# Moving two groups of transposes ahead of a matmul level in a bidirectional state scan

## The chip, the cores and the metric

The kernel runs on one core of a Trainium2 chip. The metric is the device time of one execution in microseconds. The kernel before takes 1659.57 us (median of three executions, 1650.67 to 1659.82).

## What is computed

Two transformer-like blocks follow each other on 512 tokens of width 1024, in float32. The change touches only the first block's mixer. That mixer holds a recurrence of the RWKV kind over 8 heads of width 64, run forwards and backwards over the tokens, after 256 context tokens have gone through the same recurrence:

```
def wkv_scan(state0, r, decay, kk, b, v, k, reverse):
    def step(S, inp):
        r_t, w_t, kk_t, b_t, v_t, k_t = inp
        sa = jnp.einsum("bhvk,bhk->bhv", S, kk_t)
        S = (S * w_t[:, :, None, :] - sa[..., None] * b_t[:, :, None, :]
             + v_t[..., None] * k_t[:, :, None, :])
        return S, jnp.einsum("bhvk,bhk->bhv", S, r_t)
```

Everything else (modulation, norms, the projections, two gated feed-forward networks with depthwise convolutions, and in the second block a gated linear recurrence and a sliding-window attention) is the same in both kernels.

## The kernel before, in words

The program is written by hand for each engine: TensorE (PE), VectorE (DVE), ScalarE (ACT), GpSimd (POOL) and SyncE each have one list of instructions in program order, and semaphores stand between them. Nothing reorders these lists.

The recurrence is computed in chunks of L = 64 tokens: NCC = 4 chunks of context and NCX = 8 of the sequence, NC = 12 in all, in two directions d = 0 and 1 that don't depend on each other. Within a chunk a 64 x 64 triangular system has to be inverted. That is done by doubling: levels l = 2 to 6, each of them a short chain that goes back and forth between PE and DVE:

- `nx(m, d, l)`: 8 matmuls of 64x64 by 64x32 (16 MATMUL instructions in the trace, since a float32 product is issued as two), which wait for X of the level before;
- `w_out(m, d, l)`: DVE masks the product from PSUM into w (L2214);
- `dx(m, d, l)`: again 16 MATMUL instructions, which wait for w and Y;
- `x_out(m, d, l)` (L2221): DVE adds the product to X, and `x_turned(m, d, l)` (L2228) transposes X into Y. The next level's `nx` waits for X alone, its `dx` for Y and w.

The loop at the centre of the change is `for n in range(-2, NC)`, which each engine's list contains. In iteration n three chunks are in work: chunk n is finished (`state_in`, `updates`, `state_terms`, from chunk NCC on `results`), chunk m = n + 1 is inverted (the levels), and chunk q = n + 2 is prepared (`scores_b`, `scores_k`). In iterations -1 to 6 a piece of another computation runs beside it, a matrix-vector product for the modulation: `ada_parts` (L967, 64 MATMUL instructions on the whole array), a copy by ACT, `ada_select` (L978, 8 MATMUL instructions) and one DVE addition into `mod` (L2305).

`turned(m, d)` transposes chunk m's two 64 x 64 blocks per head, `bh` and `kh`, by 16 matmuls against the identity (32 MATMUL instructions, out<-in `bank<-k_,arena`). It waits for `kr` of chunk m, which DVE wrote in the iteration before. Its results are copied by ACT (`tok_out`, L1575) and are used by `state_terms` in the next iteration. POOL may overwrite `bh` and `kh` with chunk q's only after `turned(m, d)` (`done("tok_mm", d, q)`): POOL's L1944 makes the new `bh` in two steps, L1930 multiplies `bh` and, from chunk 4 on, `rt`; `scores_b(q, d)` waits for both.

On PE, iteration n has this order around the change (level 3 only; the next level begins with `nx(m, d, 4)`):

```
state_terms(n, 0), state_terms(n, 1)
nx(m, 0, 3), nx(m, 1, 3)
turned(m, 0)
dx(m, 0, 3), dx(m, 1, 3)
ada_select(n)                      # n = -1 to 6
turned(m, 1)
results(n, 0), results(n, 1)       # n = 4 to 11
nx(m, 0, 4), nx(m, 1, 4), dx(m, 0, 4), dx(m, 1, 4), nx(m, 0, 5), nx(m, 1, 5)
```

`turned` exists for m = 0 to 10, which is n = -1 to 9; in n = 10 level 3 already stands without it. Levels 4 and 5 have no other work between `nx(4)`, `dx(4)` and `nx(5)`. On DVE, `state_out(n)` (L2264, L2266), which adds the state terms and waits for `state_terms`, stands ahead of `w_out(m, d, 3)`.

In iterations 0 to 7 SyncE also issues the weight pieces of `ada_parts`, paced by waits for the counts of `nx` and `dx` of direction 0.

Of the kernel before, what the change touches and what calls it, by code (L numbers as in the profile page):

```python
# [32 lines left out]
NC = NCC + NCX  # L33
# [137 lines left out]
def two_blocks(nc, xT, ctxT, vec, con, band, w8, w11, lora, gup, outT):  # L171
    with ExitStack() as ctx:
# [88 lines left out]
        def vcol(name, *shape):  # L261
            o, w = VEC[name]
            a = v[:, o:o + w]
            if not shape:
                return a
            names = " ".join(f"d{i}" for i in range(len(shape)))
            return a.rearrange(f"p ({names}) -> p {names}", **{f"d{i}": n for i, n in enumerate(shape)})
# [9 lines left out]
        def spread(a, *shape):  # L277

            return a.unsqueeze(len(a.shape)).broadcast_to([P, *shape])
# [305 lines left out]
        def _(pe):  # L585
# [185 lines left out]
            def done(name, d, count):  # L771

                if count > 0:
                    pe.wait_ge(s[f"{name}{d}"], count)
# [93 lines left out]
            def turned(m, d):  # L868

                sc = scans[d]  # L870
                done("kr", d, m + 1)
                for k, src in enumerate((sc.bh, sc.kh)):
                    last = tiles(lambda j, r: bank[d][1][r, NJ * L * k + L * j:NJ * L * k + L * j + L],
                                 lambda j, r: src[r, j, :], lambda j, r: ident[r, r])
                last.then_inc(s[f"tok_mm{d}"], 1)
# [23 lines left out]
            def state_terms(n, d):  # L899

                sc = scans[d]
                done("gu", d, 2 * n + 2)
                done("tok", d, n + 1)
                v_in = v_tok[:, place(d, n) // L]
                for j in range(NJ):
                    out = bank[d][3][:, L * j:L * j + L]
                    for r in HALVES:
                        mm(out[r], sc.tok[r, 0, j, :], sc.gu[r, j, :], start=True, stop=False)  # L908
                    for r in HALVES:
                        last = mm(out[r], sc.tok[r, 1, j, :], v_in[r, j, :], start=False, stop=True)  # L910
                last.then_inc(s[f"ds_mm{d}"], 1)
# [60 lines left out]
            def ada_select(n):  # L972

                pe.wait_ge(s["ada_row"], 8 + n + 2)
                done("nr", 1, n + 2)
                for u in range(2):
                    for c in range(2):
                        last = mm(banks[4][:, 4 * u + 2 * c:4 * u + 2 * c + 2], ada_row2[:, u, :], select[:, c, :],  # L978
                                  start=True, stop=True)
                last.then_inc(s["ada_turned"], 1)  # L980

            both = (0, 1)
            for n in range(-2, NC):
                m, q = n + 1, n + 2
                inv, prep, ada = 0 <= m < NC, q < NC, -1 <= n < 7
                if n >= 0:
                    for d in both:
                        state_in(n, d)
                if inv:
                    for d in both:  # L990
                        nx(m, d, 2)
                if n >= 0:
                    for d in both:
                        updates(n, d)
                if inv:
                    for d in both:
                        dx(m, d, 2)
                if ada:
                    ada_parts(n)
                if 0 <= n < NC - 1:  # L1000
                    for d in both:
                        state_terms(n, d)
                if inv:
                    for d in both:
                        nx(m, d, 3)
                if 0 <= m < NC - 1:
                    turned(m, 0)
                if inv:
                    for d in both:
                        dx(m, d, 3)  # L1010
                if ada:
                    ada_select(n)
                if 0 <= m < NC - 1:
                    turned(m, 1)
                if n >= NCC:
                    for d in both:
                        results(n, d)
                if inv:
                    for d in both:
                        nx(m, d, 4)  # L1020
                    for d in both:
                        dx(m, d, 4)
                    for d in both:
                        nx(m, d, 5)
                if prep:
                    for d in both:
                        scores_b(q, d)
                if inv:
                    for d in both:
                        dx(m, d, 5)  # L1030
                if prep:
                    scores_k(q, 0)
                if inv:
                    for d in both:
                        nx(m, d, 6)
                if prep:
                    scores_k(q, 1)
                if inv:
                    for d in both:
                        dx(m, d, 6)  # L1040
# [966 lines left out]
        def _(dve):  # L2007
# [182 lines left out]
            def done(name, d, count):  # L2190

                if count > 0:
                    dve.wait_ge(s[f"{name}{d}"], count)
# [22 lines left out]
            def x_out(m, d, l):  # L2216
                sc = scans[d]
                done("dx_mm", d, 5 * m + l - 1)
                add = bank[d][2][:, 128:256].rearrange("p (b t) -> p b t", t=1 << l - 1)
                early = sides(sc.X, l, d)  # L2220
                V.tensor_tensor(early, add, early, ALU.add).then_inc(s[f"X{d}"], 1)  # L2221

            def x_turned(m, d, l):
                sc = scans[d]
                done("X", d, 5 * m + l)
                if l == 2:
                    done("gu_mm", d, 2 * m)
                V.transpose(flat(sc.Y), flat(sc.X)).then_inc(s[f"Y{d}"], 1)  # L2228
# [48 lines left out]
            both = (0, 1)  # L2277
            dve.wait_ge(s["gate"], 2 * NJ)
            dve.wait_ge(s["presets"], 8)
            for n in range(-2, NC):  # L2280
                m, q = n + 1, n + 2
                inv, prep, ada = 0 <= m < NC, q < NC, -1 <= n < 7
                if inv:
                    for d in both:
                        w_out(m, d, 2)
                if prep:
                    for d in both:
                        running_sums(q, d)
                if inv:
                    for d in both:  # L2290
                        x_out(m, d, 2)
                        x_turned(m, d, 2)
                if 0 <= n < NC - 1:
                    state_out(n)
                if inv:
                    for d in both:
                        w_out(m, d, 3)
                if inv:
                    for d in both:
                        x_out(m, d, 3)  # L2300
                        x_turned(m, d, 3)
                if ada:
                    at = 16 + 4 * (n + 1)
                    dve.wait_ge(s["ada_turned"], n + 3)
                    V.tensor_tensor(mod[:, at:at + 4, :], banks[4][:, 0:8].rearrange("p (m c) -> p m c", c=2),  # L2305
                                    spread(vcol("adab")[:, at:at + 4], 4, 2), ALU.add).then_inc(s["mod"], 1)
                if n >= NCC + NCX // 2:
                    for d in both:
                        second_result(n, d)
                if inv:  # L2310
                    for d in both:
                        w_out(m, d, 4)
                    for d in both:
                        x_out(m, d, 4)
                        x_turned(m, d, 4)
                    for d in both:
                        w_out(m, d, 5)
                if prep and q >= NCC:
                    for d in both:
                        scores_out(q, d, 0)  # L2320
                if inv:
                    for d in both:
                        x_out(m, d, 5)
                    for d in both:
                        x_turned(m, d, 5)
                if prep:
                    for d in both:
                        first_level(q, d)
                if inv:
                    for d in both:  # L2330
                        w_out(m, d, 6)
                if prep:
                    for d in both:
                        first_turned(q, d)
                    scores_out(q, 0, 1)
                if inv:
                    for d in both:
                        y_last(m, d)
                if prep:
                    scores_out(q, 1, 1)  # L2340
# [483 lines left out]
```

## Time and profile before

| | |
|---|---|
| Device time, median of 3 | 1659.57 us |
| Lowest and highest of the 3 | 1650.67 and 1659.82 us |
| The profiled execution's own time | 1659.57 us |
| Its span in the profile | 1657.6 us |
| Scan loop (n = -2 to 11) in the trace | about 268 to 560 us |
| Mean granted TensorE clock over the span | 0.962 of full speed |

The span is what the profile covers, first to last instruction; the execution's own time is 2.0 us longer. A matmul's row starts when it is issued and ends when its last result is modelled to be out, so matmuls overlap: a small matmul's row here lasts about 0.22 us while the next one starts some 0.03 us later. A TensorE that is shown busy can therefore still lose a tenth of a microsecond between two instructions, and such losses are read from how long a given count of instructions takes. The granted clock is given as a share of full speed, 0.50 or 1.00 at any moment.

### The profile page before, as it was taken

The numbers are of one execution on the slowest core, as the hardware profiler recorded it, in microseconds if no ns is written. First come the engines' busy times: TensorE is split into PE (matmuls) and PEld (weight loads), VectorE is DVE, ScalarE is ACT, GpSimd is POOL, SyncE is SP. The second block draws the span as 40 slices with busy tenths as digits, with TensorE's granted clock in tenths as the row PEclk, the third lists the DMA queues.
The fourth block names the chain that finished last, engine by engine and source line by source line (L and its number), as shares of the span: only waits on it lengthen the run. The fifth ranks groups of instructions, "written<-read, shape, count | busy, mean of one in ns | idle before, by whom it ended". The sixth has DMA issues, their size and how long they took to land.

```text
span 1657.6 us, 36556 instructions
## 1 busy us (share of the span) xinstructions
PE 1571.5 (95%) x15540; PEld 1324.2 (80%) x15540; DVE 885.0 (53%) x1417; ACT 572.7 (35%) x987; POOL 219.5 (13%) x230
## 2 busy tenths in 40 slices
PE   7899998999999978999999999999979999999997
PEld 3787886999999766778777887777867788888886
DVE  1624213665566445888887224667454556555222
ACT  3422334332232223434443223535544222323221
POOL 0000002333233010111111121000001011111111
PEclk8899997999999988999999998999979999999999
DMA  8242100332210121222222232221102222222221
GB/s 340 77 147 77 51 26 8 99 106 92 81 42 4 53 77 52 98 79 102 101 81 107 88 104 76 82 79 57 46 26 98 80 93 86 100 101 95 90 102 68
DMA packets 38750, 139.74 MB, mean 84 GB/s; under 512 B 3040, under 2 KB 3552, under 8 KB 38112
## 3 DMA queue, kind: packets, MB, share of 16 engines
q1 hardware_dynamic: 38480, 135.76, 23.4%
q8 instruction: 104, 1.70, 0.4%
q10 hardware_dynamic: 144, 2.10, 0.3%
q14 instruction: 22, 0.18, 0.0%
HBM read 135.75 MB, written 2.10 MB: 83 GB/s over the span
## 4 chain that ended last, share of the span: by engine, by line
PE 86%; DVE 8%; ACT 3%; issue 1%; DMA 0%; POOL 0%; DVEq 0%; SPq 0%; ACTq 0%
PE bank L647 58%; PE bank L780 12%; DVE ffn_sb L2471 2%; PE bank L657 2%; PE bank L967 1%; PE bank L610 1%; PE bank L886 1%; PE bank L908 1%; PE bank L888 1%; PE bank L592 1%; PE bank L1285 1%; PE bank L910 1%; ACT arena L1752 1%; DVE w_in L2091 1%; PE bank L1256 1%
## 5 line engine op out<-in xcount | busy, mean ns | idle before, releaser
L647 PE MATMUL bank<-hf_hi,w_up 128*128 128x512 f32 x1376 | 424.9, 390 | 0.0
L647 PEld LDWEIGHTS bank<-hf_hi,w_up 128*128 128x128 f32 x1376 | 259.1, 188 | 53.6
L647 PE MATMUL bank<-hf_lo,w_up 128*128 128x512 f32 x688 | 271.2, 394 | 4.8 <-DVE w_up L2091 4.3
L647 PE MATMUL bank<-act_hi,w_down 128*128 128x512 f32 x704 | 216.8, 389 | 0.0
L780 PE MATMUL bank<-arena 64*64 64x32 f32 (+2 forms) x4992 | 177.0, 227 | 8.5 <-POOL arena L1930 7.6
L780 PEld LDWEIGHTS bank<-arena 64*64 64x64 f32 x4992 | 170.6, 137 | 13.2 <-issue 8.7
L1403 ACT ACTIVATE w_up<-ring 128x1024 fp32r<-128x1024 f32 x88 | 93.0, 1058 | 215.9 <-PE bank L647 215.9
L2091 DVE TENSOR_TENSOR w_up<-ring,w_up 128x1024 fp32r<-128x1024 f32 x88 | 108.0, 1229 | 105.3 <-ACT w_up L1403 105.2
L647 PEld LDWEIGHTS bank<-hf_lo,w_up 128*128 128x128 f32 x688 | 129.5, 188 | 39.4 <-DVE w_up L2091 13.2
L2471 DVE SCALAR_TENSOR_TENSOR ffn_sb<-ffn_sb 128x512 f32<-128x512 f32 x176 | 151.5, 861 | 5.5
L647 PEld LDWEIGHTS bank<-act_hi,w_down 128*128 128x128 f32 x704 | 132.2, 188 | 27.4
L647 PE MATMUL bank<-act_lo,w_down 128*128 128x512 f32 x352 | 137.1, 389 | 1.3 <-DVE w_down L2097 1.3
L2091 DVE TENSOR_TENSOR w_in<-ring,w_in 128x1024 fp32r<-128x1024 f32 x48 | 58.5, 1223 | 139.9 <-ACT w_in L1403 139.7
L1988 POOL TENSOR_TENSOR act_lo<-ffn_sb,act_hi 128x512 f32 x44 | 72.9, 1656 | 443.5 <-ACT act_hi L1681 429.8
L647 PE MATMUL bank<-hx_hi,w_in 128*128 128x512 f32 x384 | 120.4, 395 | 0.0
L647 PE MATMUL bank<-h_hi,w_in 128*128 128x512 f32 x320 | 98.8, 390 | 0.0
L2097 DVE TENSOR_TENSOR w_down<-ring,w_down 128x1408 fp32r<-128x1408 f32 x32 | 52.1, 1628 | 86.8 <-ACT w_down L1420 86.8
L1403 ACT ACTIVATE w_in<-ring 128x1024 fp32r<-128x1024 f32 x48 | 50.4, 1055 | 138.9 <-PE bank L647 130.9
L1420 ACT ACTIVATE w_down<-ring 128x1408 fp32r<-128x1408 f32 x32 | 44.2, 1381 | 155.6 <-PE bank L647 155.6
L647 PEld LDWEIGHTS bank<-hx_hi,w_in 128*128 128x128 f32 x384 | 73.7, 192 | 15.3
L647 PE MATMUL bank<-hx_lo,w_in 128*128 128x512 f32 x192 | 76.7, 400 | 5.4 <-ACT arena L1478 3.6
L647 PEld LDWEIGHTS bank<-act_lo,w_down 128*128 128x128 f32 x352 | 66.1, 188 | 15.4 <-DVE w_down L2097 1.8
(319 smaller groups left out, 2364.8 us busy)
## 6 DMA issues: line engine op xcount, KB each, us to landing
ring<-w SPq DMA_DIRECT2D x76, 1024.0 KB, 4.7
ring<-w SPq DMA_DIRECT2D x32, 704.0 KB, 4.0
ring<-w SPq DMA_DIRECT2D x64, 256.0 KB, 2.9
arena<-w SPq DMA_DIRECT2D x2, 3072.0 KB, 22.6
x<-xT SPq DMA_DIRECT2D x1, 2048.0 KB, 11.8
arena<-w SPq DMA_DIRECT2D x2, 1024.0 KB, 20.3
x<-xT ACTq DMA_DIRECT2D x1, 2048.0 KB, 8.9
outT<-x SPq DMA_DIRECT2D x4, 512.0 KB, 2.7
```

The costliest lines, as they stand in the source:

```text
L592: last = mm(out[32 * q:32 * q + 32, :].rearrange("r (c m) -> r c m", c=2), siluc[:, 2 * q + k, :], w[:, :, 2 * q + k, :], start=k == 0, st ...
L610: last = mm(bank[:, 0:t], ones, sq[:, k, :], start=k == 0, stop=k == KB - 1)
L647: ins = mm(out, w[:, a, k, :], of_block(b, k0 + k), start=first and k == 0 and m == 0, stop=last and k == n - 1 and m == 2)
L657: ins = mm(out, w[:, a, k, :], of_block(b, k), start=k == 0 and m == 0, stop=k == KB - 1 and m == 2)
L780: last = mm(out(j, r), lhs(j, r), rhs(j, r), start=True, stop=True)
L886: mm(out[r], sc.ktrt[r, n % 3, j, 0:L], sc.S[r, n % 2, j, :], start=True, stop=False)
L1403: act_f(w[:, 0], slot_view(g)[:, at:at + blocks, :], ACT.Copy).then_inc(s["w_hi"], 1)
L1420: act_f(w_down[half][:, 0], slot_view(g, HALF), ACT.Copy).then_inc(s["w_hi"], 1)
L1988: nc.gpsimd.tensor_tensor(act_lo[:, bass.ds(j, 1), :].rearrange("p a t -> p (a t)"), silu[u], act_hi[:, bass.ds(j, 1), :].rearrange("p a t ...
L2091: V.tensor_tensor(w[:, 1], slot_view(SLOT[name] + u)[:, c * KB:c * KB + KB, :], w[:, 0], ALU.subtract).then_inc(s["w_lo"], 1)
L2097: V.tensor_tensor(w[:, 1], slot_view(SLOT[name] + half, HALF), w[:, 0], ALU.subtract).then_inc(s["w_lo"], 1)
L2471: ins = V.scalar_tensor_tensor(to, pad[u][:, n // 3:n // 3 + GRID_H, n % 3:n % 3 + GRID_W], tap_w[u][:, n:n + 1], to, ALU.mult, ALU.add)
```

## The change

On PE both `turned` groups now stand ahead of `nx(m, d, 3)`, and `ada_select` stands between `nx(m, 1, 3)` and `dx(m, 0, 3)`. On DVE the addition into `mod`, which waits for `ada_select`, moves ahead of `x_out(m, d, 3)` accordingly. Nothing is added or removed; no wait is changed.

```
--- before.py
+++ after.py
@@ -1000,18 +1000,17 @@
                 if 0 <= n < NC - 1:
                     for d in both:
                         state_terms(n, d)
+                if 0 <= m < NC - 1:
+                    for d in both:
+                        turned(m, d)
                 if inv:
                     for d in both:
                         nx(m, d, 3)
-                if 0 <= m < NC - 1:
-                    turned(m, 0)
-                if inv:
-                    for d in both:
-                        dx(m, d, 3)
                 if ada:
                     ada_select(n)
-                if 0 <= m < NC - 1:
-                    turned(m, 1)
+                if inv:
+                    for d in both:
+                        dx(m, d, 3)
                 if n >= NCC:
                     for d in both:
                         results(n, d)
@@ -2295,15 +2294,15 @@
                 if inv:
                     for d in both:
                         w_out(m, d, 3)
-                if inv:
-                    for d in both:
-                        x_out(m, d, 3)
-                        x_turned(m, d, 3)
                 if ada:
                     at = 16 + 4 * (n + 1)
                     dve.wait_ge(s["ada_turned"], n + 3)
                     V.tensor_tensor(mod[:, at:at + 4, :], banks[4][:, 0:8].rearrange("p (m c) -> p m c", c=2),
                                     spread(vcol("adab")[:, at:at + 4], 4, 2), ALU.add).then_inc(s["mod"], 1)
+                if inv:
+                    for d in both:
+                        x_out(m, d, 3)
+                        x_turned(m, d, 3)
```

The list of PE in iteration n = 0, from the end of `state_terms` (L908 and L910) to the `state_in` after it. `bank<-arena 64x32` rows are `nx` and `dx` (8 matmuls a direction), `bank<-k_,arena` is `turned`, L978 is `ada_select`, the last two `64x64` and `64x32` rows belong to `scores` and the later levels:

```order
 L908 MATMUL bank<-arena 64x64 x2
 L910 MATMUL bank<-x,arena 64x64 x2
-L780 MATMUL bank<-arena 64x32 x16
-L780 MATMUL bank<-k_,arena 64x64 x16
+L780 MATMUL bank<-k_,arena 64x64 x32
 L780 MATMUL bank<-arena 64x32 x16
 L978 MATMUL bank<-k_,x 128x2 x4
-L780 MATMUL bank<-k_,arena 64x64 x16
-L780 MATMUL bank<-arena 64x32 x48
+L780 MATMUL bank<-arena 64x32 x64
 L780 MATMUL bank<-arena 64x64 x16
 L780 MATMUL bank<-arena 64x32 x16
```

Both transpose groups (x16 each) now stand as one x32 ahead of level 3. Between `nx(3)` and `dx(3)` there is `ada_select`, and from `dx(3)` on 64 matmuls of the levels stand in one row, with nothing between `dx(3)`, `nx(4)`, `dx(4)` and `nx(5)`.

The list of PE in iteration n = 7, which has no `ada_select` but has `results` (L923 and on), in the kernel before:

```order
L780 MATMUL bank<-arena 64x32 x16
L780 MATMUL bank<-k_,arena 64x64 x16
L780 MATMUL bank<-arena 64x32 x16
L780 MATMUL bank<-k_,arena 64x64 x16
L923 MATMUL bank<-arena 64x64 x2
```

and in the kernel after:

```order
L780 MATMUL bank<-k_,arena 64x64 x32
L780 MATMUL bank<-arena 64x32 x32
L923 MATMUL bank<-arena 64x64 x2
```

Here `nx(3)` and `dx(3)` have become one row of 32 with nothing between them; `results` still follows `dx(3)`.

The list of DVE in an iteration with `ada`, from `w_out(3)` to `w_out(4)`, in the kernel before (line 2305 is the addition into `mod`):

```order
L2214 TENSOR_TENSOR arena<-bank,k_ 128x128 [waits nx_mm0]
L2214 TENSOR_TENSOR arena<-bank,k_ 128x128 [waits nx_mm1]
L2221 TENSOR_TENSOR arena<-bank,arena 128x32x4 [waits dx_mm0]
L2228 STREAM_TRANSPOSE arena<-arena 128x256 [waits X0]
L2221 TENSOR_TENSOR arena<-bank,arena 128x32x4 [waits dx_mm1]
L2228 STREAM_TRANSPOSE arena<-arena 128x256 [waits X1]
L2305 TENSOR_TENSOR mod<-bank,v 128x8 [waits ada_turned]
L2214 TENSOR_TENSOR arena<-bank,k_ 128x128 [waits nx_mm0]
```

and in the kernel after (its lines are one to five lower in number):

```order
L2213 TENSOR_TENSOR arena<-bank,k_ 128x128 [waits nx_mm0]
L2213 TENSOR_TENSOR arena<-bank,k_ 128x128 [waits nx_mm1]
L2300 TENSOR_TENSOR mod<-bank,v 128x8 [waits ada_turned]
L2220 TENSOR_TENSOR arena<-bank,arena 128x32x4 [waits dx_mm0]
L2227 STREAM_TRANSPOSE arena<-arena 128x256 [waits X0]
L2220 TENSOR_TENSOR arena<-bank,arena 128x32x4 [waits dx_mm1]
L2227 STREAM_TRANSPOSE arena<-arena 128x256 [waits X1]
L2213 TENSOR_TENSOR arena<-bank,k_ 128x128 [waits nx_mm0]
```

The addition into `mod` went from behind level 3's transposes to ahead of its `x_out`. ACT's, POOL's and SyncE's lists are the same in both kernels.

## Rows read from the trace of the kernel before

**Rows 1.** The page's first lines: span, busy time by engine.

```profile
span 1657.6 us, 36556 instructions
...
PE 1571.5 (95%) x15540; PEld 1324.2 (80%) x15540; DVE 885.0 (53%) x1417; ACT 572.7 (35%) x987; POOL 219.5 (13%) x230
```

**Rows 2.** The page's chain that ended last, by engine.

```profile
PE 86%; DVE 8%; ACT 3%; issue 1%; DMA 0%; POOL 0%; DVEq 0%; SPq 0%; ACTq 0%
```

**Rows 3.** Windows: whole scan, iterations n = 0, 7 and 10.

```profile
core 0: us, PE busy (x) PEld busy (x) DVE busy (x) ACT busy (x) POOL busy (x), PEclk, DMA share, GB/s
268.00:560.00 292.00, 283.06 (x8512) 276.22 (x8512) 174.62 (x509) 91.21 (x266) 93.54 (x136) 0.97 0.19 62
299.80:321.33 21.53, 21.53 (x687) 20.92 (x685) 13.13 (x43) 7.95 (x23) 6.97 (x10) 1.00 0.32 103
467.60:490.18 22.58, 22.58 (x712) 22.39 (x710) 14.83 (x43) 7.32 (x22) 8.20 (x12) 1.00 0.06 16
535.50:557.00 21.50, 21.00 (x682) 20.31 (x680) 11.78 (x37) 2.68 (x7) 0.00 (x0) 1.00 0.02 5
```

**Rows 4.** Waits of PE in the scan, 268 to 560 us.

```profile
PE bank L780 <- POOL arena L1930: 7.6, 2, 6.9
```

**Rows 5.** Timeline of iteration n = 0, PE and DVE: start, us, instruction, [idle before].

```profile
308.38 1.07 PE L780 MATMUL bank<-arena 64*64 64x32 f32 x32
...
309.06 0.42 DVE L2266 TENSOR_TENSOR arena<-arena 128x256 f32<-128x256 f32 x1
...
309.40 0.48 DVE L2214 TENSOR_TENSOR arena<-bank,k_ 128x128 f32<-128x128 f32 x2
...
311.25 1.05 PE L978 MATMUL bank<-k_,x 128*128 128x2 f32 x8
...
312.35 0.17 DVE L2305 TENSOR_TENSOR mod<-bank,v 128x8 f32<-128x8 f32 x1
...
313.87 0.29 DVE L2214 TENSOR_TENSOR arena<-bank,k_ 128x128 f32<-128x128 f32 x1 [1.36 <-PE bank L780]
...
314.34 0.29 DVE L2214 TENSOR_TENSOR arena<-bank,k_ 128x128 f32<-128x128 f32 x1 [0.17 <-PE bank L780]
...
314.92 0.29 DVE L2221 TENSOR_TENSOR arena<-bank,arena 128x128 f32<-128x128 f32 x1 [0.29 <-PE bank L780]
315.25 0.45 DVE L2228 STREAM_TRANSPOSE arena<-arena 128x256 f32<-128x256 f32 x1
315.62 0.25 DVE L2221 TENSOR_TENSOR arena<-bank,arena 128x128 f32<-128x128 f32 x1
...
315.91 0.45 DVE L2228 STREAM_TRANSPOSE arena<-arena 128x256 f32<-128x256 f32 x1
316.27 0.65 DVE L2214 TENSOR_TENSOR arena<-bank,k_ 128x128 f32<-128x128 f32 x2
```

**Rows 6.** Windows of PE: level 3, then levels 4 and 5; n = 0, 2, 7.

```profile
core 0: us, PE busy (x), PEclk, DMA share, GB/s
308.36:311.12 2.76, 2.76 (x104) 1.00 0.30 99
313.20:316.39 3.19, 3.19 (x104) 1.00 0.33 116
356.77:360.10 3.33, 3.33 (x104) 1.00 0.37 125
474.17:476.93 2.76, 2.76 (x103) 1.00 0.03 9
480.70:483.88 3.18, 3.18 (x104) 1.00 0.02 5
```

**Rows 7.** Timeline of POOL in iteration n = 2.

```profile
357.05 0.73 POOL L1944 TENSOR_TENSOR arena<-arena 128x256 f32<-128x256 f32 x1 [2.24 <-PE bank L780]
357.86 2.69 POOL L1930 TENSOR_TENSOR arena<-arena 128x256 f32<-128x256 f32 x4
```

**Rows 8.** Windows of PE, n = 10: level 3, then `nx(4)` and `dx(4)`.

```profile
541.90:544.20 2.30, 2.02 (x72) 1.00 0.00 0
547.04:549.00 1.96, 1.96 (x72) 1.00 0.03 8
```

**Rows 9.** Windows at the low clock: start of the scan, and later.

```profile
279.30:282.83 3.53, 3.53 (x70) 3.48 (x66) 2.29 (x6) 0.58 (x3) 0.16 (x1) 0.50 0.02 5
...
1199.00:1209.00 10.00, 9.25 (x43) 8.02 (x43) 4.66 (x14) 9.25 (x17) 0.00 (x0) 0.50 0.01 2
```

More of the change, by code:

```diff
@@ L1005, in _ @@
                         nx(m, d, 3)
-                if 0 <= m < NC - 1:
-                    turned(m, 0)
+                if ada:
+                    ada_select(n)
                 if inv:
@@ L1010, in _ @@
                         dx(m, d, 3)
-                if ada:
-                    ada_select(n)
-                if 0 <= m < NC - 1:
-                    turned(m, 1)
                 if n >= NCC:
```

## The prediction

> **What bounds the kernel now.** I read the page's first lines, then the chain that ended last, then the scan alone in windows, then one iteration instruction by instruction. TensorE is shown busy for 1571.5 of 1657.6 us [rows 1] and holds 86% of the chain that ended last [rows 2]; VectorE, busy for 53%, holds 8%. The change lies in the scan, 268 to 560 us, where TensorE is busy for 283.06 of 292.00 us; iterations n = 0 and n = 7 show it busy for their whole 21.53 and 22.58 us, at a granted clock of 1.00 [rows 3]. The list of waits in the scan has one large entry, 7.6 us for POOL in two waits, one of them 6.9 us [rows 4]. This stands at the scan's start, before the first `turned`, and the change doesn't touch it. So the scan goes at the pace of TensorE's list. A change of order can win only what TensorE loses between instructions, and that does not show as idle time, since a matmul's row outlasts its issue by 0.2 us. It has to be read from how long equal counts of instructions take.
>
> There the profile is clear. In n = 0 the 96 instructions of level 3 (`nx`, `turned(m, 0)`, `dx`) take 2.76 us; the 96 of `nx(4)`, `dx(4)`, `nx(5)`, which have nothing between them, take 3.19 us [rows 6] (both windows count 104, since 8 earlier rows reach in). Iteration 7 gives 2.76 and 3.18 us. At 2.76/96 = 0.029 us an instruction, the covered level loses nothing, and the uncovered stretch loses 0.43 us in three joints. Level 3 is already covered today; the transposes cannot be a better cover for it than they are. What they leave, they uncover.
>
> **What an uncovered joint costs.** VectorE's rows in n = 0 split the 0.43 us [rows 5]. The two `w_out(4)` start at 313.87 and 314.34, 0.47 us apart, which is one direction's 16 instructions. The two `x_out(4)` start at 314.92 and 315.62, 0.70 us apart, because direction 0's transpose (315.25, 0.45 us) stands between them. `nx(5)` of direction 1 waits for the second, which ends at 315.87, 0.66 us after the first ended at 315.21. Its turn on TensorE would come after 0.47 us, so 0.19 us is lost there. The other 0.43 - 0.19 = 0.24 us is the way PE to DVE and back, once after `nx(4)` and once after `dx(4)`: 0.12 us each. So a bare joint from `nx` to `dx` costs 0.12 us, and a bare joint from `dx` to the next `nx` costs 0.12 + 0.19 = 0.31 us.
>
> **The change part by part.**
>
> *`nx(3)` to `dx(3)`.* Before, `turned(m, 0)` stood there. After, in n = -1 to 6 `ada_select` does: it takes about 1.0 us (its row starts at 311.25, the next group's work follows one microsecond later) [rows 5], against the 0.12 us that has to be covered. Nothing is lost, 8 times. In n = 7, 8 and 9 nothing stands there: 3 x 0.12 = +0.36 us. In n = 10 there was no `turned`, and nothing changes.
>
> *`dx(3)` to `nx(4)`.* Before, `ada_select` and `turned(m, 1)` stood there. After, from n = 4 on `results` does, 96 instructions or about 2.8 us by the rate above: covered. In n = -1 to 3 nothing does: 5 x 0.31 = +1.55 us.
>
> *`nx(4)` to `dx(4)` in the same five iterations.* VectorE now comes to `w_out(4)` from level 3's transposes without a break. What that is like stands in the rows one level on [rows 5]: after the transpose at 315.91 the next `w_out` starts at 316.27, 0.65 us after `x_out` of direction 1 began at 315.62. `nx` of that direction starts at about 315.93 (0.06 us after 315.87) and takes 0.47 us, so TensorE is free at 316.40; the first mask is done at 316.27 + 0.29 = 316.56, and with 0.06 us to TensorE `dx` could start at 316.62. There `scores_b` hides this; at level 4 it would show 0.22 us in place of 0.12. Five times 0.10 makes +0.50 us, and the rest of level 4 is as before.
>
> *The transposes themselves.* They cost the same instructions. Their wait, `kr` of chunk m, was fulfilled in the iteration before. In their new place they delay `nx(3)` by 64 x 0.029 = 1.9 us, which nobody but the levels waits for. `state_out` on VectorE, which ends at 309.48 in n = 0 (309.06 + 0.42) right when `w_out(3)` begins [rows 5], now lies under the transposes; there was no stall behind it to win, since level 3 took 2.76 us.
>
> *POOL.* The new `bh` needs both transposes done. `turned(m, 1)` moves about 3 us earlier (the 16 + 16 instructions of `nx` and of `dx` and `ada_select`: 0.93 + 0.93 + 1.0 us), so POOL's work for the next chunk ends earlier. This wins in n = 2 and 3 alone, where `rt` is wanted and no `results` gives POOL time: in n = 2 POOL takes up direction 1's `bh` at 357.05 and is in its four multiplications until 360.55 [rows 7], and the stretch up to `scores_b` takes 3.33 us in place of 3.19 [rows 6]. 2 x 0.14 = -0.28 us.
>
> *The addition into `mod` on VectorE.* It took 0.17 us at 312.35, right after `ada_select` [rows 5]. In its new place it is done while `dx(3)` of direction 0 is still issuing (0.47 us). Behind it wait `x_out(3)` and so `nx(4)`; they need `dx(3)`, which comes later anyway. Cost nothing; it would cost up to 0.17 us in each of 8 iterations, 1.4 us, if that cover were missing.
>
> *SyncE.* Two of the eight paced pieces in an iteration wait for `nx` or `dx` of level 3 and go out about 2 us later; the last ones wait for level 6 and go as before. As the slots are wanted only after the last, nothing.
>
> Sum: 0.36 + 1.55 + 0.50 - 0.28 = +2.1 us. The profiled execution took 1659.57 us, which is also the median of the three; its span is 1657.6 and 2.0 us lie around it. So 1659.57 + 2.1 = 1661.7 us.
>
> Bounds. Below: if no joint shows and only POOL's gain does, -0.3 us. Above: n = 10 is the worst joint of this level in the trace. There `nx(3)` and `dx(3)` stand bare behind `state_terms` and the same 64 instructions take 2.30 us in place of 1.96 for level 4's, which itself loses 0.12 [rows 8], so 0.46 us. If each of the 8 iterations with a new bare joint cost 0.46 at `nx` to `dx`, on top of 0.31 + 0.10 in five of them, it would be 3.7 + 2.0 = +5.7 us. I take the 0.12, because in n = 10 VectorE is held up by `state_out`, and after the change 1.9 us of transposes stand between. With the 1.4 us of the addition, +7.1 us is the upper end.
>
> **The rivals.**
>
> *Only the gain shows.* For it: the waits are tenths of a microsecond, and the profile's list shows none of them. Against it: rows 6 show the loss at levels 4 and 5 in each iteration that I looked at. Time: 1659.3 us.
>
> *The clock falls, and it is slower.* TensorE's rows in n = -1 to 3 would break more often, and if its granted clock fell to the low of its two levels (1.2 in place of 2.4 GHz) there, an instruction of the scan would take 3.53 us for 64 (0.055 us) in place of 0.029 [rows 9]. Later in the kernel such a stretch lasts at least from 1199 to 1209 us [rows 9]; 10 us of it holds work for about 5.3, so it costs 4.7 us. One in each of the five iterations makes +23.5 + 2.1 us: 1685 us. It decides from four such stretches on: 18.8 + 2.1 is over 1%. Against it: iteration 10 has the 0.46 us stall and 0.5 us of idle time in 21.50, and its clock reads 1.00 [rows 3], as do all those with levels 4 and 5 bare.
>
> The Trainium skill speaks for this rival (page "TensorE: Matmul & The Clock Gate", section "A second HAM failure mode: psum-queue depth-cycling"): where TensorE idles for moments between groups of matmuls often enough, its clock goes back and forth and the throughput suffers. This trace bears it out for this kernel's scan so far in no iteration: the clock is 1.00 in rows 3 with three such joints in each. By that rule the time would be this rival's.
>
> *The runs' own spread.* One execution of three was 8.9 us shorter than the other two. The low clock in some later stretches [rows 9] can fall otherwise when the scan ends 2 us later. If the lower value becomes the usual one: 1650.7 + 2.1 = 1652.8 us.
>
> *More is won than I see, over 1%.* For that TensorE would have to lose 16.6 us over 11 iterations, 1.5 us in each, at the places that are now filled. Level 3 took 2.76 us for 96 instructions, as fast as the list can go. I find no room for it.
>
> **How the numbers follow.** My case has 0.77, the lower value of the spread 0.12, only the gain 0.05, the clock 0.03, the upper bound near 1667 another 0.03. The likeliest case gives 1661.7 us. For 8 in 10 the range must hold my case with its bounds (1659.3 to 1666.7), and reach down to the lower value: 1652 to 1667 us. About 1% (16.6 us) is what a measurement of this kernel can tell from no change. Faster by over 1% (under 1643): 0.01. Slower by over 1% (over 1676): 0.04, the clock and what I overlook. The same: 0.95.
>
> **What would show it right or wrong.** Right: in n = 0 to 3 the 64 instructions from `dx(3)` to `nx(5)` show a bare joint more, seen in VectorE's second `x_out(3)` starting 0.7 us after the first, and in `w_out(4)` right behind the second transpose; those iterations get 0.3 to 0.45 us longer, n = 4 to 6 stay, n = 7 to 9 get 0.12 longer, and n = 2's stretch up to `scores_b` loses its extra 0.14 us. POOL's L1944 of direction 1 comes about 3 us earlier. Wrong: a granted clock under 1.00 between 290 and 555 us; VectorE's addition into `mod` ending after `dx(3)` of direction 0; `dx(3)` of n = 7 waiting longer than 0.15 us; or the scan getting shorter.

## The result, and the profile after

The changed kernel takes 1675.7 us (median of four executions, 1670.06 to 1682.14), beside 1658.67 us for the kernel before in the same comparison. The ratio is 1.0111, with a 95% interval of 1.0072 to 1.0151: about 1.1% slower, outside the range that I gave. Over all of its 35 executions it took between 1663.97 and 1686.08 us, with a median of 1674.9.

The page of the changed kernel, its first lines and its chain by engine:

```profile
span 1672.3 us, 36556 instructions
...
PE 1585.7 (95%) x15540; PEld 1337.8 (80%) x15540; DVE 888.0 (53%) x1417; ACT 573.6 (34%) x987; POOL 219.4 (13%) x230
...
PE 89%; DVE 7%; ACT 3%; issue 1%; DMA 0%; POOL 0%; SPq 0%; DVEq 0%; ACTq 0%
```

Against [rows 1, 2] the span grew by 14.7 us and TensorE's busy time by 14.2 us, with the same 15540 instructions. So it is not TensorE's shown idle time that grew. Either its instructions take longer, or there are more of the short waits that hide inside its rows. The list of TensorE's waits in the scan shows no new one, since its large entry is that of [rows 4]:

```profile
PE bank L780 <- POOL arena L1929: 7.6, 2, 6.9
```

The iterations n = -1 to 8 of the changed kernel, in windows of PE (us, busy with its count, granted clock, DMA):

```profile
279.79:302.15 22.36, 22.36 (x524) 0.72 0.27 83
302.15:326.47 24.32, 24.32 (x687) 0.86 0.29 89
326.47:352.57 26.10, 26.01 (x686) 0.80 0.27 84
352.57:378.74 26.17, 26.17 (x686) 0.87 0.28 86
378.74:402.00 23.26, 23.26 (x686) 1.00 0.32 95
402.00:427.69 25.69, 25.69 (x783) 1.00 0.27 86
427.69:453.37 25.68, 25.68 (x782) 1.00 0.28 86
453.37:481.02 27.65, 27.58 (x782) 0.94 0.27 79
481.02:504.18 23.16, 23.02 (x710) 1.00 0.06 16
504.18:526.88 22.70, 22.70 (x710) 1.00 0.02 4
```

and of the kernel before, n = -1 to 3 and n = 8:

```profile
279.35:299.82 20.47, 20.47 (x524) 0.80 0.28 91
299.82:321.36 21.54, 21.54 (x687) 1.00 0.32 103
321.36:343.12 21.76, 21.72 (x687) 1.00 0.31 100
343.12:366.41 23.29, 23.29 (x687) 1.00 0.29 95
366.41:389.45 23.04, 23.04 (x688) 1.00 0.29 95
...
490.20:512.78 22.58, 22.58 (x710) 1.00 0.02 5
```

The reader should look at the clock. In n = 0, 1 and 2 it was 1.00 and is 0.86, 0.80 and 0.87, and these three iterations got 2.8, 4.3 and 2.9 us longer; n = -1 went from 0.80 to 0.72 and got 1.9 us longer. Where the clock stayed at 1.00, the change costs what the waits cost: +0.22 us in n = 3 and +0.12 us in n = 8. The four iterations n = -1 to 2 hold 11.9 of the 14.7 us. Of the later ones, n = 6, with a clock of 0.94, takes 27.65 us against 25.68, n = 7 takes 0.6 us more at a clock of 1.00, and n = 4 takes 25.69 where the kernel before takes 26.80, of which TensorE is shown idle for 0.54.

Windows just before such a fall and behind it, in n = 0 and n = 1 of the changed kernel:

```profile
314.00:316.00 2.00, 2.00 (x52) 1.95 (x51) 0.86 (x4) 2.00 (x7) 1.73 (x3) 1.00 0.47 139
316.30:323.00 6.70, 6.70 (x126) 6.70 (x128) 2.92 (x9) 0.77 (x2) 1.90 (x3) 0.50 0.49 157
338.00:340.00 2.00, 2.00 (x46) 1.94 (x43) 0.75 (x3) 2.00 (x7) 1.92 (x4) 1.00 0.34 89
340.30:350.20 9.90, 9.90 (x190) 9.90 (x190) 4.95 (x16) 1.26 (x4) 2.29 (x4) 0.50 0.40 122
```

TensorE was shown busy throughout, at the high of its two levels, with `ada_select`, `dx(3)` and the start of `nx(4)` in n = 0, and with `nx(3)`, `ada_select` and the start of `dx(3)` in n = 1. Then the clock was at the low one for 7 and 10 us, while it went through the rest of levels 3 to 6. In n = 1 the fall comes before the iteration's new bare joint: the clock is low from 340.1 us on, and `nx(4)` has to wait for `x_out(3)`, which begins at 340.21:

```profile
340.00:340.10 0.10, 0.10 (x10) 0.92 0.49 184
340.10:340.20 0.10, 0.10 (x10) 0.50 0.43 164
...
340.21 0.29 DVE L2220 TENSOR_TENSOR arena<-bank,arena 128x128 f32<-128x128 f32 x1 [0.43 <-PE bank L780]
```

The waits themselves came as worked out. VectorE in n = 3, whose clock was 1.00:

```profile
389.83 0.29 DVE L2213 TENSOR_TENSOR arena<-bank,k_ 128x128 f32<-128x128 f32 x1 [1.42 <-PE bank L780]
390.29 0.29 DVE L2213 TENSOR_TENSOR arena<-bank,k_ 128x128 f32<-128x128 f32 x1 [0.18 <-PE bank L780]
391.27 0.17 DVE L2300 TENSOR_TENSOR mod<-bank,v 128x8 f32<-128x8 f32 x1 [0.68 <-PE bank L978]
391.86 0.29 DVE L2220 TENSOR_TENSOR arena<-bank,arena 128x128 f32<-128x128 f32 x1 [0.43 <-PE bank L780]
392.19 0.45 DVE L2227 STREAM_TRANSPOSE arena<-arena 128x256 f32<-128x256 f32 x1
392.56 0.25 DVE L2220 TENSOR_TENSOR arena<-bank,arena 128x128 f32<-128x128 f32 x1
392.84 0.45 DVE L2227 STREAM_TRANSPOSE arena<-arena 128x256 f32<-128x256 f32 x1
393.21 0.65 DVE L2213 TENSOR_TENSOR arena<-bank,k_ 128x128 f32<-128x128 f32 x2
```

The addition into `mod` (391.27) ends before `x_out(3)` begins, the two `x_out(3)` stand 0.70 us apart (391.86 and 392.56), and `w_out(4)` follows the second transpose at 393.21, 0.65 us after that `x_out`. POOL came earlier, in n = 2 of the changed kernel:

```profile
363.26 0.73 POOL L1943 TENSOR_TENSOR arena<-arena 128x256 f32<-128x256 f32 x1 [0.21 <-PE bank L780]
364.07 2.68 POOL L1929 TENSOR_TENSOR arena<-arena 128x256 f32<-128x256 f32 x4
```

That is 10.7 us after the iteration's start at 352.57, where [rows 7] had 13.9 us after 343.12: 3.2 us earlier.

### The profile page after: what moved, and what is told of

The parts are those of the page before. It is cut to its first block, busy times and chain, and to the rows that moved or that the text cites. A ratio compares the mean times of both kernels' runs of the same rounds, so it can differ in the third digit from the quotient of the medians.

```text
span 1672.3 us, 36556 instructions
## 1 busy us (share of the span) xinstructions
PE 1585.7 (95%) x15540; PEld 1337.8 (80%) x15540; DVE 888.0 (53%) x1417; ACT 573.6 (34%) x987; POOL 219.4 (13%) x230
## 4 chain that ended last, share of the span: by engine, by line
PE 89%; DVE 7%; ACT 3%; issue 1%; DMA 0%; POOL 0%; SPq 0%; DVEq 0%; ACTq 0%
PE bank L647 60%; PE bank L780 12%; PE bank L657 2%; PE bank L967 1%; DVE ffn_sb L2470 1%; PE bank L610 1%; PE bank L886 1%; PE bank L908 1%; PE bank L888 1%; PE bank L592 1%; PE bank L910 1%; PE bank L1284 1%; ACT arena L1751 1%; DVE w_in L2090 1%; PE bank L800 1%
## 5 line engine op out<-in xcount | busy, mean ns | idle before, releaser
L780 PE MATMUL bank<-arena 64*64 64x32 f32 (+2 forms) x4992 | 190.8, 236 | 8.2 <-POOL arena L1929 7.6
L780 PEld LDWEIGHTS bank<-arena 64*64 64x64 f32 x4992 | 184.6, 147 | 12.6 <-issue 7.7
L1929 POOL TENSOR_TENSOR arena<-arena 128x256 f32<-128x256 f32 x88 | 60.1, 708 | 172.6 <-ACT arena L1564 138.1
```

What stands on the lines that cost most here:

```text
L780: last = mm(out(j, r), lhs(j, r), rhs(j, r), start=True, stop=True)
L1929: nc.gpsimd.tensor_tensor(to, a, b, ALU.mult).then_inc(s[f"{name}{d}"], 1)
```

## The experiments

Two theories about the low clock, and one about the place, were tried. **A**: TensorE's added waits bring it. **B**: what TensorE works on brings it: the long row of light matmuls (32 columns, and `ada_select`'s 2) from which the 64-column transposes were taken away. **C**: the time is lost in n = 7 to 9.

**1. The new order in n = -1 to 3 alone, and from n = 4 on alone.**

```
-                if 0 <= m < NC - 1: ...
+                if n < NCC:      # e1_first; e2_later: n >= NCC
+                    (the changed kernel's order, on PE and on DVE)
+                else:
+                    (the order of before)
```

> The new order only in n = -1 to 3, the old one from n = 4 on. Theory A (TensorE's added waits at bare joints bring its granted clock down) and theory B (the long row of light instructions, 2-column ada_select and 32-column levels without the 64-column transposes among them, brings it down) both place the loss in these five iterations: 1670 to 1680 us, low clock in each of them. Theory C (the loss comes from n = 7 to 9, bare between nx(3) and dx(3)): 1658 to 1661 us.

> The complement of e1_first: the old order in n = -1 to 3, the new one from n = 4 on. The only added waits are 3 x 0.1 us in n = 7 to 9. If the loss belongs to n = -1 to 3 alone: as the kernel before, 1658 to 1661 us, ratio below 1.003. If the later iterations lose too (the changed kernel's trace shows one low stretch at 473 us, in n = 6): 1662 to 1666 us.

Measured: e1_first 1673.95 us, ratio 1.0089 (1.0060 to 1.0117); e2_later 1664.57 us, ratio 1.0019 (0.9996 to 1.0042). Nearly all of the loss belongs to the first five iterations, and C falls. A small loss in the later ones is not shown by the times, nor excluded. The profile of e2_later has a low stretch in n = 6 (27.23 us at a clock of 0.94), as both profiles of the changed kernel have and that of the kernel before has not.

**2. Which transposes have to stay where.** Three other orders, each with all transposes and no instruction more (`turned0` stands for `turned(m, 0)`, `[results]` for `results` from n = 4 on):

```
 e3_second_back:    turned0          nx3   ada_select   dx3   turned1      [results]   nx4
 e4_select_covers:                   nx3   turned0,1    dx3   ada_select   [results]   nx4
 e8_both_late:                       nx3   ada_select   dx3   turned0,1    [results]   nx4
```

> As the changed kernel, but turned(m, 1) goes back between dx(3) and nx(4); turned(m, 0) stays ahead of nx(3). No joint is bare in n = -1 to 3 that wasn't before. A and B: clock 1.00 in n = 0 to 3, 1658 to 1661 us. If instead merely moving the transposes ahead of level 3 (turned(m, 0) and the later nx(3)) brings the clock down: 1668 us or more.

> Both transposes between nx(3) and dx(3); ada_select alone (1.0 us, light work of 2 columns) between dx(3) and nx(4). No added wait, but the row dx(3), ada_select, nx(4), dx(4), nx(5) holds no transposes. A: clock 1.00 in n = 0 to 3, 1658 to 1661 us. B: the clock falls there as in the changed kernel, 1670 to 1680 us.

> Both transposes between dx(3) and nx(4), ada_select between nx(3) and dx(3); in n = 7 to 9 the joint nx(3) to dx(3) is bare. The added waits are 3 x 0.12 us, and the row from nx(4) on is as long as in the kernel before. A and B: clock 1.00 from n = 0 on, 1658 to 1662 us. If any move of the transposes away from the middle of level 3 brings the clock down: 1670 us.

Measured: e3_second_back 1662.11 us, 1.0011 (0.9986 to 1.0035); e4_select_covers 1670.95 us, 1.0084 (1.0051 to 1.0117); e8_both_late 1661.78 us, 1.0026 (1.0008 to 1.0045). e4_select_covers is the telling one. Between e4 and the kernel before only `turned(m, 1)` changed its place, and it uncovers no joint: `ada_select` stands for 1.0 us between `dx(3)` and `nx(4)`. VectorE in its n = 0 had level 3's second transpose done before TensorE's `nx(4)` was, and waited for TensorE at `w_out(4)` (316.00), not the other way round:

```profile
314.95 0.45 DVE L2227 STREAM_TRANSPOSE arena<-arena 128x256 f32<-128x256 f32 x1
315.41 0.17 DVE L2304 TENSOR_TENSOR mod<-bank,v 128x8 f32<-128x8 f32 x1
316.00 0.29 DVE L2213 TENSOR_TENSOR arena<-bank,k_ 128x128 f32<-128x128 f32 x1 [0.43 <-PE bank L780]
```

Yet its clock fell in n = 1, 2 and 3 (the first line is n = 0):

```profile
301.95:323.78 21.83, 21.57 (x687) 1.00 0.33 103
323.78:349.62 25.84, 25.83 (x688) 0.82 0.28 86
349.62:375.90 26.28, 26.28 (x684) 0.86 0.27 83
375.90:401.78 25.88, 25.88 (x688) 0.87 0.28 85
```

A alone cannot explain this. In the two orders that lost least (e3, e8), a transpose stands right ahead of `nx(4)`, as in the kernel before. Neither is quite free of loss. In the profile of e3 the clock is 1.00 in n = 0 to 3, but at the low level for 10 us in n = -1 (291.5 to 301.9 us). e8 is 2.8 us slower with an interval clear of 1, and half of that is waits: each of its n = 7, 8 and 9 takes 23.05 us in place of 22.58. There `nx(3)` to `dx(3)` is bare right behind `state_terms` and costs 0.47 us, where the changed kernel, with both transposes ahead, loses 0.12. That is the stall of n = 10 which the prediction took as its upper bound; it expected 0.12 because the transposes would stand between, and the two runs bear that out.

**3. The bare joint filled, by heavy and by light work.** The changed kernel with 32 MATMUL instructions more in n = -1 to 3, whose result nobody reads:

```
                 if inv:
                     for d in both:
                         dx(m, d, 3)
+                if 0 <= m <= NCC:
+                    for d in both:
+                        tiles(lambda j, r: bank[d][3][r, L * j:L * j + L],
+                              lambda j, r: scans[d].nr[r, m % 2, j, 0:L], lambda j, r: ident[r, r])
```

e6_light has `L * j + 32` and `ident[r, r][:, 0:32]` in place of the full width.

> The changed kernel with 32 more MATMUL instructions of 64 columns (0.93 us, nobody reads them) between dx(3) and nx(4) in n = -1 to 3, where nothing stands now. By work alone, with the clock at 1.00: 1662 + 5 x (0.93 - 0.31 - 0.10) = 1664.6 us. Theory B (transposes or other 64-column work must stand in the row of levels) and theory A (the added wait matters) both say that, with no low clock from n = 0 on. If neither holds: 1675 us or more.

> The same with 32 columns in place of 64, the same count of instructions and the same 0.93 us: the joint is covered, but by light work. A: as e6_heavy, 1664 to 1665 us. B: the clock falls as in the changed kernel, 1672 to 1682 us.

Measured: e6_heavy 1667.6 us, 1.0063 (1.0045 to 1.0081); e6_light 1677.28 us, 1.0112 (1.0078 to 1.0146). The median of the granted clock over each one's eight executions is 0.9615 and 0.9525 (the kernel before has 0.963 beside them). Both fill the same joint with the same count of instructions, and the waits are the same: n = 3, with a clock of 1.00 in both profiles, takes 23.82 us in either. The single executions overlap (1662.36 to 1674.61 us, and 1662.81 to 1684.08), but seven of the eight heavy ones lie under 1670 us and seven of the eight light ones above it. The heavy filling gives back most of the clock, the light one next to nothing. The time of e6_heavy is 3 us above what I expected, so it doesn't give back all.

**4. `ada_select` out of the row.** The changed kernel with `ada_select` ahead of both transposes:

```
+                if ada:
+                    ada_select(n)
                 if 0 <= m < NC - 1:
                     for d in both:
                         turned(m, d)
                 if inv:
                     for d in both:
                         nx(m, d, 3)
-                if ada:
-                    ada_select(n)
```

> The changed kernel with ada_select ahead of the transposes, so that it is no part of the row of levels and the joint nx(3) to dx(3) is bare as well (5 x 0.12 us more of waits in n = -1 to 3, and 3 x 0.12 in n = 4 to 6). If ada_select, 2 columns wide, is what makes the row too light: clock 1.00 from n = 0 on, about 1663 us. If the levels' own 32-column work and the waits do it: low clock as in the changed kernel, 1672 to 1680 us.

Measured: 1668.88 us, 1.0058 (1.0035 to 1.0080), median clock 0.9575. This lies between the two answers: about half of the loss goes with `ada_select`'s place, though the joint from `nx(3)` to `dx(3)` is now bare too. I had allowed for one or the other.

**5. Waits alone, on the kernel before.** Its order is untouched; `nx(m, d, 5)` waits longer than it needs in n = -1 to 3:

```
                 done("X", d, 5 * m + l - 1)
+                if l == 5 and m <= NCC:
+                    done("Y", d, 5 * m + 3)
+                    done("Y", 1 - d, 5 * m + 3)      # e10_wait_both alone
```

> The kernel before with nx(m, d, 5) waiting for Y (the transposed X) and not X alone, in n = -1 to 3: some 0.5 us more of TensorE's waiting per iteration, as much as the changed kernel has, with its order of instructions untouched. A: the clock falls in these iterations, 1668 to 1680 us. B: clock 1.00 there and only the waits themselves, 5 x 0.5 us: 1661 to 1663 us.

> As e5_longer_wait, but nx(m, d, 5) in n = -1 to 3 waits for both directions' Y: about 1.2 us more of waiting than the kernel before in each of the five iterations (the changed kernel has 0.36), order of work untouched. Waits themselves: 5 x 1.2 = 6 us, 1665 us with the clock as before. If waits bring the clock down as the light row of work does: 1678 us or more.

Measured: e5_longer_wait 1664.38 us, 1.0025 (1.0007 to 1.0044); e10_wait_both 1668.75 us, 1.0062 (1.0038 to 1.0087); median clock 0.960 in both, against 0.963. Ahead stood 2.5 and 6 us for the waits themselves, which would leave 2 us in either for the clock. That e10 waits as meant is seen on VectorE in n = 0:

```profile
316.05 0.29 DVE L2224 TENSOR_TENSOR arena<-bank,arena 128x128 f32<-128x128 f32 x1 [0.29 <-PE bank L780]
...
318.31 0.29 DVE L2217 TENSOR_TENSOR arena<-bank,k_ 128x128 f32<-128x128 f32 x1 [0.84 <-PE bank L780]
```

From `x_out(4)` to `w_out(5)` it takes 2.26 us, where [rows 5] have 1.35 (314.92 to 316.27): 0.9 us more, and VectorE waits for TensorE, which had waited for both transposes. Five times 0.9 is 4.5 us and not 6, so up to 4 us of e10's 8.3 may be the clock. Waits therefore do bring low clock. In the profile of e10 it was at the low level for 3.5 us in each of n = 0, 1 and 2, each time from within a microsecond behind the added wait on (318.2 us in n = 0); in that of e5, which is the slowest of its ten executions, for 17 us in n = 0 to 2. But it is the smaller part. At `nx(5)` of n = 3 TensorE is shown idle for 0.50 us in e5 and 1.16 us in e10, where the changed kernel adds 0.41 us of waits by the prediction's sum; and either lost about a quarter of what the changed kernel lost at the clock (0.960 against 0.951).

**6. The changed kernel again.**

> The changed kernel once more, unaltered, for a second profile and a second set of times. If the low clock belongs to the order of work: low stretches again in n = -1 to 3, beginning in levels 3 to 5, 20 to 35 us more of low clock in the scan than the kernel before, ratio 1.008 to 1.013. If the first profile was chance: low stretches elsewhere in the scan or few.

Measured: 1671.96 us, 1.0083 (1.0050 to 1.0116). Its second profile has a granted clock of 0.86 in the 120 us from 290 to 410 us; the first has 0.87 there and the kernel before 1.00:

```profile
290.00:410.00 120.00, 119.78 (x3181) 0.86 0.29 91
```

The falls are no chance of one profile, but their places vary: the second profile has them in n = 0 to 3, 5 and 6. One profile of a kernel is one draw, so for each run the clock of this stretch is set beside the time of the execution that was profiled and the run's median (the kernel before had medians of 1658.7 to 1660.4 us beside them):

| Run | Clock, 290 to 410 us | Profiled execution, us | Median, us |
|---|---|---|---|
| kernel before | 1.00 | 1659.57 | 1658.67 |
| changed kernel | 0.87 | 1674.32 | 1675.7 |
| e11_changed_again | 0.86 | 1679.33 | 1671.96 |
| e1_first | 0.87 | 1671.35 | 1673.95 |
| e4_select_covers | 0.87 | 1670.95 | 1670.95 |
| e7_select_early | 0.94 | 1675.39 | 1668.88 |
| e6_light | 0.96 | 1670.58 | 1677.28 |
| e5_longer_wait | 0.93 | 1674.72 | 1664.38 |
| e10_wait_both | 0.96 | 1669.68 | 1668.75 |
| e3_second_back | 0.96 | 1660.01 | 1662.11 |
| e6_heavy | 1.00 | 1662.36 | 1667.6 |
| e2_later | 1.00 | 1665.57 | 1664.57 |
| e8_both_late | 1.00 | 1657.77 | 1661.78 |

**7. A faster order.** The kernel before, with `results` moved from n = 4 on, and `second_result` on VectorE with it (only PE's part for n = 4 to 9 is shown; in n = 10 `results(n, 0)` goes between `nx(3)` and `dx(3)`, and `results(n, 1)` stays behind `dx(3)`):

```
                     for d in both:
                         nx(m, d, 4)
+                    if n >= NCC and m < NC - 1:      # written with a flag in the kernel
+                        results(n, 0)
                     for d in both:
                         dx(m, d, 4)
+                    if n >= NCC and m < NC - 1:
+                        results(n, 1)
                     for d in both:
                         nx(m, d, 5)
```

> A try at a faster kernel: the old order, but from n = 4 on results(n, 0) stands between nx(4) and dx(4) and results(n, 1) between dx(4) and nx(5) (in n = 10 between nx(3) and dx(3), and behind dx(3)), so that the joints of level 4 are covered by 64-column work. By the waits removed: 6 x 0.36 + 0.45 = 2.6 us less than before; the clock as before or better. 1656 to 1657 us, ratio about 0.9985.

Measured: 1658.3 us beside 1660.44, ratio 0.9987 (0.9970 to 1.0003), as expected, and too little to tell from no change. Its iterations do show the gain:

```profile
491.13:513.29 22.16, 22.16 (x711) 1.00 0.02 5
...
535.45:555.21 19.76, 19.50 (x583) 0.89 0.02 4
```

n = 8 takes 22.16 us in place of 22.58. But n = 10 takes 19.76 in place of 18.38, as its clock fell to 0.89 in this profile; there the transposes are missing, and half of `results` was moved away from ahead of level 4. Whether that is why it fell was not tried.

## Why the prediction was wrong

**The sum of the waits held.** In n = 3 I had 0.41 - 0.14 = +0.27 us, and the trace shows +0.22; in n = 8 I had 0.12 and it shows 0.12. The rows of VectorE and POOL came out within 0.1 to 0.3 us of what I had written. By itself this sum is 2.1 us. The gain from POOL in n = 2 can't be read, since the clock was 0.87 there.

**The step that failed is the weight of the rival on the clock.** My case took the clock to stay at 1.00 in n = -1 to 3, a term of 0 us, and gave the rival that it falls there a chance of 0.03. It happened, and the term is about 13 us: with the mean granted clock of 0.951, 2 x (1 - 0.951) x 1673 = 164 us of an execution pass at the low level; with 0.9625 in the kernel before it is 2 x 0.0375 x 1658 = 124 us. That is 40 us more, and the time that the waits don't explain is 1674.9 - 1659.9 - 2.1 = 13 us (1659.9 us and 0.9625 are the medians of 20 executions). In n = 1 a clock of 0.80 over 26.10 us makes 10.4 us at the low level, and the iteration lost 4.34 - 0.41 = 3.9 us beyond its waits: 0.38 us for each. I had priced it at 0.47. A likely reason, by estimate, is that I took the full-clock rate of covered work, 0.029 us an instruction; with the waits of bare joints it is 3.19/96 = 0.033, and (0.055 - 0.033)/0.055 = 0.40. The rival's 1685 us also took 10 us in each of five iterations; the first profile has 7, 10 and 7 in n = 0 to 2, 7 in n = -1, none in n = 3 and 3.5 in n = 6.

**Why I weighed it wrongly.** Against it I put that n = 10 and the bare levels 4 and 5 keep a clock of 1.00. That is an argument on waits, and on waits it was partly right: in e5_longer_wait, with about as much added waiting as the changed kernel, they cost an estimated 2 us beyond themselves. What I didn't look at is what stands between the levels. "They cost the same instructions" was true of the transposes' time and said nothing of what they do for the clock where they stand. The change took the 64-column work out of the middle of a row of 32-column work and put 2-column work at its head; e4_select_covers (no wait added) and e6_light against e6_heavy (the same waits) show that this matters. In n = 10, `results` (64 columns, 2.8 us) stood ahead of `nx(4)`: my counterexample held just such work.

By the Trainium skill's rule that I had cited (page "TensorE: Matmul & The Clock Gate", section "A second HAM failure mode: psum-queue depth-cycling") the clock should go back and forth when TensorE idles for moments between groups. The clock did go back and forth, so the trace agrees with its outcome; its cause covers e5 and e10, but not e4, where the clock fell with no wait added.

**The other rivals.** Only the gain, and more won than I saw: both no. The runs' own spread: the kernel before varies between 1650.7 and 1666.8 us over all of its executions, without steps, and its medians in the five comparisons are 1658.7 to 1660.4; that explains nothing of 15 us. Its breadth also says that my 8.9 us "lower value" was no second level.

**What stays open.** How the clock's fall depends on the mix in detail stays open: e7 puts about half of it on `ada_select`, and e6_heavy doesn't return all. Whether it is the columns or another property of those instructions was tried with one pair of widths only. In n = -1 the clock fell a second time even in e3, with a transpose right ahead of `nx(4)`. The place of the falls is read from one profile of each kernel, two for the changed one.

## What to carry to other kernels

In a stretch of small matmuls, an order of instructions with the same count and the same waits can still change the time, since the granted clock depends on what TensorE has been doing. Before light groups are placed side by side, look whether the clock already falls anywhere near, as it did here at the start of the scan, and weigh the heavier groups not only as cover for a wait but by what stands around them. When a profile after shows more busy time on the same instructions, read the clock by stage first.

## What the runs showed of the hardware

The granted clock fell from 1.00 to 0.50 for 7 to 10 us at a time while TensorE was shown busy for all of the 2.00 us ahead of it, working on groups of 2 and 32 columns (short waits between instructions don't show in its rows). A filling of 32 instructions with 64 columns kept the median clock at 0.9615, the same filling with 32 columns left it at 0.9525. With the order untouched, about 0.9 us of added waiting in each of five iterations (e10_wait_both) cost 8.3 us, more than the 4.5 us of the waits, and brought the median clock from 0.963 to 0.960. A microsecond at the low level cost 0.38 us in n = 1 of this scan, less than half.
